# A mixture-of-experts layer on one NeuronCore: the expert stages as one loop of uniform items, with expert outputs written to rows of their own and summed afterwards

## The reference

```
# D 1024, 64 experts, TOP_K 8, expert width 256; layer 0: 768 tokens, layer 1: 512
top_idx, top_w = route(xf, w_router, b_router)        # 8 experts and 8 weights a token
# assignments are sorted by expert and padded to blocks of 128 rows
def body(acc, blk):
    tok, w, e = blk
    xb = x_pad[tok]
    h = jax.nn.silu(xb @ w_gate[e]) * (xb @ w_up[e])
    return acc.at[tok].add((h @ w_down[e]) * w[:, None]), None
# result: routed + shared, where shared = (silu(xf @ ws_gate) * (xf @ ws_up)) @ ws_down
```

## Time and profile before

| | us |
|---|---|
| three runs: median (lowest to highest) | 3462.98 (3459.09 to 3465.24) |
| span of the profiled execution | 3452.0 |
| experts of layer 0, about | 840 to 1840 |
| experts of layer 1, about | 2478 to 3423 |
| PE busy | 2794.7 (81%) |
| DVE busy | 2159.4 (63%) |
| ACT busy | 1509.0 (44%) |
| POOL busy | 1260.6 (37%) |
| DMA queue of POOL's gathers and scatters | 118.78 MB, 16.5% of 16 engines' span |

### The profile page before, as it was taken

The page is one execution under the profiler, slowest core; times in us unless marked ns, Lnnn a source line. Parts: engine busy times, 40 slices in busy tenths (PEclk is TensorE's granted clock), DMA queues, the critical chain, the costliest instruction groups (busy, mean ns, idle before and its releaser), DMA issues. The chain is left out here.

```text
span 3452.0 us, 46471 instructions
## 1 busy us (share of the span) xinstructions
PE 2794.7 (81%) x12826; PEld 2105.5 (61%) x12827; DVE 2159.4 (63%) x2406; ACT 1509.0 (44%) x2033; POOL 1260.6 (37%) x856
## 2 busy tenths in 40 slices
PE   8899999877888888778882788867788877888884
PEld 2266677754666676566661677756476656666663
DVE  7733345436666657878764465543667878778884
ACT  5521334312555545555552233322255655555552
POOL 1000000111555546555564000002165655556554
PEclk9999999988989999999995999988899999998997
DMA  9820100232898888999982111002489999889994
GB/s 357 316 74 5 37 1 1 71 135 107 252 275 268 252 228 260 294 289 291 287 236 88 56 38 37 19 5 113 186 245 280 273 287 285 267 270 271 278 286 133
DMA packets 206943, 643.04 MB, mean 186 GB/s; under 512 B 30664, under 2 KB 41928, under 8 KB 206336
## 3 DMA queue, kind: packets, MB, share of 16 engines
q1 hardware_dynamic: 162464, 518.83, 42.9%
q0 software_dynamic: 43232, 118.78, 16.5%
q10 hardware_dynamic: 1152, 4.19, 0.3%
HBM read 587.06 MB, written 90.28 MB: 196 GB/s over the span
## 5 line engine op out<-in xcount | busy, mean ns | idle before, releaser
L1590 DVE TENSOR_TENSOR F_gu_lo<-gu_raw,F_gu_hi 128x2048 fp32r<-128x2048 f32 x256 | 996.6, 3932 | 178.4 <-ACT F_gu_hi L1524 177.0
L1404 POOL TENSOR_TENSOR F_d_lo<-d_raw,F_d_hi 128x2048 fp32r<-128x2048 f32 x128 | 657.6, 5138 | 0.0
L101 PE MATMUL F_psG<-F_gu_hi,F_xT_hi 128*128 128x512 f32 x1152 | 506.7, 440 | 76.6 <-DVE F_xT_lo L1582 74.0
L102 PE MATMUL F_psG<-F_gu_lo,F_xT_hi 128*128 128x512 f32 x1152 | 488.4, 424 | 0.0
L103 PE MATMUL F_psG<-F_gu_hi,F_xT_lo 128*128 128x512 f32 x1152 | 487.6, 423 | 0.0
L1524 ACT ACTIVATE F_gu_hi<-gu_raw 128x2048 fp32r<-128x2048 f32 x256 | 475.6, 1913 | 13.3 <-PEq L126 13.3
L101 PEld LDWEIGHTS F_psG<-F_gu_hi,F_xT_hi 128*128 128x128 f32 x1152 | 241.4, 210 | 147.1 <-issue 78.6
L1457 PE MATMUL F_psX<-cst,F_xb 128*128 128x128 f32 x1168 | 173.3, 295 | 146.6 <-DMA F_xb<-f_d,F_gi 146.2
L1409 POOL COPY F_si<-tok 128x1 int32 x144 | 83.2, 578 | 552.1 <-DMA acc_d<-F_yb,F_si 552.0
L1399 POOL DMA_INDIRECT acc_d<-F_yb,F_si x146 | 232.5, 1592 | 118.5 <-issue 93.0
L103 PEld LDWEIGHTS F_psG<-F_gu_hi,F_xT_lo 128*128 128x128 f32 x1152 | 240.0, 208 | 56.8
(11 more groups left out here) (306 smaller groups left out, 4903.5 us busy)
## 6 DMA issues: line engine op xcount, KB each, us to landing
gu_raw<-in_we_gate_dram SPq DMA_DIRECT2D x256, 512.0 KB
gu_raw<-in_we_up_dram SPq DMA_DIRECT2D x256, 512.0 KB
d_raw<-in_we_down_dram SPq DMA_DIRECT2D x256, 512.0 KB
wada<-in_w_ada_dram SPq DMA_DIRECT2D x24, 2048.0 KB, 11.0
I_w_raw<-in_wc_in_dram SPq DMA_DIRECT2D x32, 384.0 KB, 5.8
acc_d<-o SPq DMA_DIRECT2D x12, 512.0 KB, 2.6
f_d<-D_f SPq DMA_DIRECT2D x10, 512.0 KB, 2.6
H_ac<-acc_d SPq DMA_DIRECT2D x10, 512.0 KB, 8.9
```

The source lines that it names most:

```text
L101: nc.tensor.matmul(acc, xh, wh, start=(start and i == 0), stop=False)
L102: nc.tensor.matmul(acc, xh, wl, start=False, stop=False)
L1404: G.tensor_tensor(d_lo[:, j], d_raw[:, j], d_hi[:, j].bitcast(F32), ALU.subtract).then_inc(s_dl, 1)
L1590: V.tensor_tensor(gu_lo[:, j, v], gu_raw[:, j, v], gu_hi[:, j, v].bitcast(F32), ALU.subtract).then_inc(s_gul, 1)
```

## The change

1. **Items instead of blocks.** The first block of each of the 64 experts is an item, in the order of the experts; blocks beyond the first follow as items of their own, each with the number of its expert in `ctl_i`. The number of items is rounded up to an even number of at least 64. Every item loads and splits the weights of its expert, also where that expert's first block did so before. The walk is one loop over pairs of items on each engine, without branches inside; SP reads an expert's number for each item. Weights come in three DMAs of 1 MB an item, each with a semaphore of its own.
2. **Double buffers.** `xb`, `yb`, `gi` and `si` have two buffers each.
3. **Rows of their own.** The scatter no longer adds. Each assignment writes its row at token*8 + choice of `y_d`, with 8 rows a token, and padding is left out by the bound. ACT makes all of `yb` in one instruction.
4. **Low half of down on DVE.** POOL makes no halves any more.
5. **Combine** loads the 8 rows of each token (4 MB a tile of 128 tokens), sums them with a `tensor_reduce` on DVE, and then POOL multiplies by the gate and adds. **Route** multiplies the shared expert's result by the gate and adds it to `h` on POOL, in place of a store to DRAM; its table has two columns instead of three, in float32.

```
@@ stage_experts, gpsimd
-                        def take_rows(b):
-                            pool.wait_ge(s_sc, 16 * b + 16)
-                            G.tensor_copy(si[:], moe.tok[:, bass.ds(b, 1)]).then_inc(s_sidx, 1)
-                        def step(b, j, change, e, split):
-                            take_rows(b - 1)
-                            pool.wait_ge(s_tx, b + 2)
-                            gather(b + 2)
-                            give(b - 1)
-                            if split:
-                                split_down(j, e + 2)
+                        def scatter(i, j):
+                            pool.wait_ge(s_y, i + 2)
+                            G.tensor_copy(si[j][:], moe.sca[:, bass.ds(i, 1)]).then_inc(s_si, 1)
+                            pool.wait_ge(s_si, i + 3)
+                            send(j)
+                        def send(j):
+                            pool.sem_inc(s_bear, 1)
+                            pool.indirect_dma_start(y_d[l], bass.IndirectOffsetOnAxis(ap=si[j][:].bitcast(U32), axis=0), yb[:, j], None,
+                                                    bounds_check=nt * P * TOPK - 1, oob_is_err=False).then_inc(s_sc[j], 16)
+                        m = pairs_of(pool)
+                        with pool.Fori(1, m + 1) as q:
+                            for j in (1, 0):
+                                i = 2 * q - j
+                                scatter(i - 1, 1 - j)
+                                pool.wait_ge(s_tx, i + 1)
+                                gather(i + 2, j)
@@ stage_experts, tensor
+                        with pe.Fori(1, m + 2) as q:
+                            for j in (1, 0):
+                                i = 2 * q - j
+                                front(i, j)
+                                pe.wait_ge(s_x[1 - j], 16 * q + 16)
+                                turn_rows(1 - j)
+                                down_of(i - 1, 1 - j)
@@ stage_experts, scalar
+                                hidden(i - 1)
+                                split_gate_up(1 - j, 16 * q + 16)
+                                act.wait_ge(s_gu, i + 1)
+                                silu()
+                                act.wait_ge(s_tx, i + 2)
+                                rows()
+                                split_down(j, 16 * q + 16 * (1 - j))
+                                out_of(i - 1, 1 - j, 16 * q)
@@ stage_experts, vector
+                                hidden(i - 1)
+                                split_gate_up(i + 1, 1 - j)
+                                dve.wait_ge(s_sil, i + 1)
+                                product()
+                                rows(i + 1)
+                                split_down(i, j)
@@ stage_experts, sync
+                        with sp.Fori(1, m + 2) as q:
+                            for j in range(2):
+                                e = sp.value_load(ctl_i[0:1, bass.ds(2 * q + j, 1)], min_val=0, max_val=NE - 1)
+                                reload(2 * q + (j - 2), j, e)
@@ stage_combine
-                            sp.dma_start(ac[:, t % 3], acc_d[l][t * P:(t + 1) * P]).then_inc(s_ac[t % 3], 16)
+                            sp.dma_start(y8[:, t % 2], rows_of[t]).then_inc(s_ac[t % 2], 16)
+                            nc.vector.tensor_reduce(ac[:, t % 2], y8[:, t % 2].rearrange("p k d -> p d k"), AX, ALU.add).then_inc(s_sum, 1)
```

More of the change, by code:

```diff
@@ L38 @@
 FAR = 16384
+NPAIR = MAXBLK + 1
 C_ID, C_U, C_ONE, C_MP, C_MN = 0, P, 2 * P, 3 * P, 4 * P
@@ new lines, in _ @@
+                        for j in range(2):
+                            G.memset(xb[:, j], 0.0).then_inc(s_xb0, 1)
+                            G.memset(yb[:, j], 0.0).then_inc(s_xb0, 1)
+                            G.tensor_copy(si[j][:], moe.sca[:, TBL - 1:TBL]).then_inc(s_si, 1)
+                        pool.wait_ge(s_xb0, 4)
+                        pool.wait_ge(s_si, 2)
+                        for j in range(2):
+                            send(j)
+                        gather(0, 0)
+                        gather(1, 1)
@@ L1444, in last @@
+                        pool.wait_ge(s_tx, i + 1)
+                        gather(i + 2, 1)
+                        scatter(i, 1)
+                        scatter(i + 1, 0)
+                        scatter(i + 2, 1)
+                        for j in range(2):
+                            pool.wait_ge(s_sc[j], 16 * m + 48)
                             pool.sem_inc(s_bear, 1)
-                        all_steps(pool, step, last)
+                            pool.wait_ge(s_x[j], 16 * m + 32)
+                            pool.sem_inc(s_bear, 1)
@@ L1555, in step @@
-                        def step(b, j, change, e, split):
-                            hidden(b - 1)
-                            if split:
-                                act.wait_ge(s_gu, b)
-                                split_gate_up(j, e + 2)
-                            act.wait_ge(s_gu, b + 1)
-                            silu()
-                            act.wait_ge(s_tx, b + 2)
-                            rows()
-                            out_of(b - 1)
-                            if split:
-                                split_down(j, e + 2)
@@ L1568, in last, with out_of, hidden @@
-                        def last(b):
-                            hidden(b - 1)
-                            out_of(b - 1)
-                        all_steps(act, step, last)
+                        def out_of(i, j, free):
+                            act.wait_ge(s_dn, i + 1)
+                            act.wait_ge(s_sc[j], free)
+                            nc.scalar.activation(yb[:, j].rearrange("p (b n) -> p b n", b=2), psY[:], ACT.Copy, scale=moe.wgt[:, bass.ds(i, 1)]).then_inc(s_y, 1)
+                        def hidden(i):
+                            act.wait_ge(s_ht, i + 1)
+                            nc.scalar.activation(hT_hi[:], psH[:, 0:KF], ACT.Copy).then_inc(s_hTh, 1)
@@ L1574, in _ @@
+                        i = 2 * m + 3
+                        hidden(i - 1)
+                        act.wait_ge(s_gu, i + 1)
+                        silu()
+                        split_down(1, 16 * m + 32)
+                        out_of(i - 1, 0, 16 * m + 32)
+                        hidden(i)
+                        out_of(i, 1, 16 * m + 32)
                     @block.vector
@@ L1714, in _ @@
+                        for t in range(nt + 2):
+                            if t < nt:
+                                summed(t)
+                            if 1 <= t <= nt:
+                                normed(t - 1)
+                            if aT is not None and t >= 2:
+                                low(t - 2)
                     @block.gpsimd
                     def _(pool):
-                        def added(t):
-                            pool.wait_ge(s_g, t + 1)
-                            nc.gpsimd.tensor_tensor(h[:, t], h[:, t], ac[:, t % 3], ALU.add).then_inc(s_h, 1)
```

419 lines of the change are left out of this document (188 added, 231 removed).

## The result

The changed kernel takes 4,634.1 us (median of 4 runs, 4,628.9 to 4,634.8) against 3,461.0 us for the kernel before (4 runs beside it): ratio 1.338, 95% interval 1.336 to 1.340. It is slower, as forecast, but by 1,173 us instead of 685, and above the top of the range, 4,500 us. The profiled execution spans 4,632.1 us, 1,180.1 more than before.

A forecast was written before the change was run, and what follows sets the result against it. The prediction took the scatter-to-gather loop, 13.1 us a block, as the bound; the new loop's 17.0 us an item adds 589 us, combine 92, route 4, giving 4,148 us, range 3,640 to 4,500.

The forecast's parts named there:

- The loop through POOL's order: Experts: gather of i+2 stands behind scatter of i-1, which waits for that item's output; a one-item loop of 17.0 us.
- The floor by traffic: Experts: weight loads of 9.0 us plus gathered and scattered rows of 1.6 us make 10.6 us an item.
- the faster rival: Experts: double buffers hide the loop and traffic bounds, 3,226 us, or it closes with all low ends, 3,370; 7 in 100.
- The advice to double-buffer: Experts: by the skill page rows would be at hand, giving 3,226 us; the order on POOL speaks against it.
- turning to output: PE's turning of rows to start of output: 5.43 us at the lower clock, 4.0 the lower end.
- Nearer the low end: 4.8 us: Start of gather to turned rows: 4.8 us, between 3.3 at best and 8.94 in the thick of the loads.
- in the thick of the loads: Longer rival, experts: gathers land in 8.94 us, with 2.0 of holding 21.1 us an item, 4,738 us; 8 in 100.
- Holding: DVE's differences of gate and up hold POOL's `gi` copy and gather issue: 0 to 4.5 us, taken as 2.0.
- Combine: Combine stages: layer 0 105 us against 56, layer 1 72 against 29; sum +92 us.
- some 60 us: Combine: what the reduction's 4 KB stride would add at half speed; no row showed it.
- Route: Route: POOL's multiply and add, one payload product less a tile, small instructions more; between -10 and +15 us, taken as +4.
- The table is made by PE and DVE at the same pace: Route's table: the ground given for taking the route's change as +4 us.

The follow-up runs named there:

- one change of order: Changed kernel with POOL's gather of item i+2 put ahead of the scatter of item i-1: 3,325.8 us, ratio 0.961 to the kernel before.
- Small loads: Changed kernel with reloads in the loop cut to an eighth of gate and up and a quarter of down: 4,234.1 us.
- delayed loads: Changed kernel with SP holding the reload of down, and gate and up behind it, until the item's rows are turned: 3,954.4 us.
- PE kept busy: Changed kernel with 32 more matmuls of 512 columns on PE in each item, ahead of its wait for gathered rows: 4,589.9 us.

## Where the prediction was right and wrong

**The mechanism was right.** The loop through POOL's order, the wait of PE for rows with double buffers standing by, the missing scatter wait, the lengthened copies and issues are all there, and one change of order opens the loop. The floor by traffic, 10.6 us, measured 10.9 with the loop open; the faster rival's 3,226 us for that case measured 3,326, which the dearer combine and route (61 us) and 0.3 us an item about explain. The advice to double-buffer, which the prediction took from the Trainium skill's page Trainium Kernel Development and Optimization (section "Best Practices"), gave its gain only where the order let a gather run ahead.

**The sizes were wrong.** The terms of the 17.0 us beside the means of 73 periods of layer 0, from one output to the next, all those that have every part:

| term (us) | forecast | measured |
| --- | --- | --- |
| turning to output | 5.43 | 6.13 |
| output to index copy | 1.13 | 1.29 |
| `si` copy and gap | 1.45 | 1.14 |
| scatter to `gi` copy | 1.08 | 1.03 |
| `gi` copy, gap, and holds outside the gather | 3.06 | 2.98 |
| gather to turning | 4.8 | 7.78 |
| item | 16.95 | 20.36 |

- **The step that failed is "Nearer the low end: 4.8 us".** It argued that DMA would be busy for 10.6 of 17 us, and that gate and up would be reloaded only after the gather had been issued. The first is a mean over the item, and the load was not spread: all of it ran ahead of the rows and nothing after them. The second was wrong: the buffers of gate and up are free from the head of the item before, and their loads stand on SP behind the reload of down, which waits for DVE's low half of down, about when the output is made. So all three go together, ahead of the gather. Measured, the term is 7.78 us, 3.0 more than forecast and nearly the whole miss of an item; 1.2 of it is the gather's own hold. Small loads and delayed loads, each alone, took the landing to 5.4 and 4.9 us. What the forecast did name as a rival, the landing "in the thick of the loads", 21.1 us and 4,738 us, was nearer than the forecast, and had 8 in 100.
- **Turning to output**, 0.7 us too small. 5.43 was taken after a wait of 2.75 us; here PE waits 8.5 us, and the granted clock is 0.61 from the turning to the output. With PE kept busy this term fell by 1.15 us, and more than half of that was lost again to holds.
- **Holding** was forecast at 2.0 us: 1.9 in the copy and 1.2 in the issue of the gather were measured. As a size that is fair, but the sum was the wrong way to price it: in the burst the holds cost nothing, in the quiet queue they cost 1.9. The Trainium skill's page SBUF — State Buffer (section "SBUF: two separate sides", and in it "Who interferes with whom") ties the holding of descriptor writing to DVE's 2-port modes and says that `tensor_tensor` has no such mode. The trace differs, and decides: the gather's issue goes from 2.24 to 1.05 us when the plain `tensor_tensor` differences beside it are cut to a sixteenth.
- The miss in the experts is 1,024 - 589 = 435 us, 3.0 us for each of the 144 intervals; an item misses by 3.4 us in these periods, and the first and last of a layer are shorter (20.08 us from first to last turning). With 40 us in combine and 21 in route it makes up the 495 us that the forecast of the span lacked (1,180 - 685).
- **Combine**: +132 against +92, the stretch up to the next table of layer 1 included, where some 8 us lie outside the combine stage. The reduction takes 14.0 us a tile where 10.2 were taken from 768 elements without a stride, and so DVE and not the load of 4 MB sets the tile (12.9 us to landing). The stride was named as unpriced, at "some 60 us" for half speed; 3.8 us on ten tiles are 38. The sum also left out what DVE does beside the reduction: from one reduction to the next it is 18.7 us in layer 0, with 3.4 us for the normalised rows and 1.2 for their low half.

```profile
L1669 DVE TENSOR_REDUCE H_ac<-H_y 128x1024 f32<-128x8192 f32 x10 | 140.1, 14022 | 51.3 <-DMA H_y<-y_d 51.3
```

- **Route**: +25 against +4. "The table is made by PE and DVE at the same pace" overlooked the type. With float32 in place of the rounded one a tile has 16 matmuls in the trace, 3.30 us, for 8, 1.84 us. Nor did it see POOL's new multiply and add: beside them six products that give the weights take 8.01 us where they took 3.70, and DVE's first product for the table takes 3.25 us and later ones 1.12. DVE is 13 us later than before when it comes to the table:

```profile
782.11 3.70 DVE L1268 TENSOR_TENSOR o<-o,E_wt 128x512 f32<-128x512 f32 x6
...
834.21 1.84 PE L1157 MATMUL E_psS<-E_pay,E_onep 128*128 128x348 f32 x8
```

```profile
791.10 8.01 DVE L1284 TENSOR_TENSOR o<-o,E_wt 128x512 f32<-128x512 f32 x6
...
857.43 3.30 PE L1152 MATMUL E_psS<-E_pay,E_onep 128*128 128x232 f32 x16
...
808.18 3.25 DVE L1307 TENSOR_TENSOR E_pay<-o,E_tokv 128x928 f32<-128x928 f32 x1
...
814.81 1.12 DVE L1307 TENSOR_TENSOR E_pay<-o,E_tokv 128x928 f32<-128x928 f32 x1
```

The first fence is of the kernel before, the second of the changed one. No run here took the route apart, so how the 25 us divide is read from these lines and not shown.

## What to carry to other kernels

A second buffer opens a loop only if the instruction that fills it can be issued before the one that ends the item; where a queue runs in order, read its order first. When a loop closes through a transfer, lay the issue times of all transfers side by side before pricing its landing: those that start together compete, and a mean DMA share of a half can be a burst at full rate and a pause. Inside a burst the terms of such a loop do not add up: taking away 3 us of holding brought nothing here, and adding a wait that delays the bulk loads brought 15%. In the quiet queue the sum gave the total within 0.2 us an item, but not its parts.

## What the runs showed of the hardware

- A single-column copy on POOL takes 0.18 to 0.20 us alone and 2.18 beside a DVE difference of 128x2048; the issue of an indirect DMA 1.02 to 1.05 and 2.24. On the other side, the same difference on DVE takes 2.29 us, and 2.95 in the mean when POOL computes differences of its own, which take 4.63.
- A reduction over 8 rows with a stride of 4 KB runs at 14.02 us for 8,192 elements, 1.71 ns an element; contiguous additions of 4,096, 2,048 and 1,024 at 1.30, 1.61 and 1.39 ns an element in the mean, beside work on POOL.
- Beside 3 MB of loads, the first of two indirect transfers of at most 128 rows of 4 KB (70 in the mean, 10,240 in 146 items) took 8.7 us to land, and the second landed 3 us behind it; with the loads held back, 4.9 to 5.2.
